# RWKV-7 recurrence in one core's trunk kernel: head pairs stacked on partitions, each product as two 64x64 matmuls in two quarters of the array

## The reference, cut to what matters

```python
def rwkv7_scan(r, w, k, v, a, b, s0):
    def step(s, xs):
        r_t, w_t, k_t, v_t, a_t, b_t = xs
        sa = jnp.einsum('bhvk,bhk->bhv', s, a_t)
        s = s * w_t[:, :, None, :] + sa[..., None] * b_t[:, :, None, :] + v_t[..., None] * k_t[:, :, None, :]
        return s, jnp.einsum('bhvk,bhk->bhv', s, r_t)
...
decay = jnp.exp(-jnp.exp(heads(w)))
o, s = rwkv7_scan(rh, decay, kh, vh, -kk, kk * ah, s0.astype(jnp.float32))
```

## Time and profile before

| what | value |
|---|---|
| median of 3 runs | 4238.09 us (4236.41 to 4239.77) |
| span of the profiled execution | 4230.9 us |
| TensorE busy in the span | 3786.5 us, 27818 matmul records |
| VectorE, ScalarE, GpSimd busy | 1979.8, 1070.2, 1270.0 us |
| RWKV stage: first scan to last state update | 2476.49 to 3037.74 us |

### The profile page before, as it was taken

How to read it: one execution, slowest core, us unless ns; L and a number is a source line. 1 busy time by engine, 2 the same in 40 slices (tenths; PEclk the granted TensorE clock), 3 DMA queues, 4 the chain that set the end, 5 groups by cost and what they waited for, 6 DMA issues and landing times. The chain is left out here.

```text
span 4230.9 us, 67031 instructions
## 1 busy us (share of the span) xinstructions
PE 3786.5 (89%) x27818; PEld 3609.9 (85%) x27818; DVE 1979.8 (47%) x2308; ACT 1070.2 (25%) x1429; POOL 1270.0 (30%) x685
## 2 busy tenths in 40 slices
PE   8997886989999998889978768888787999999988
PEld 7987876889999998889964458888786999999978
DVE  1653553455444456444122355555425445454573
ACT  2464332121111211310133432222303211111131
POOL 3334332433333333433320011111034333333342
PEclk9999998999999999999989889999998999999989
DMA  3110001111111111022210241111120111111111
GB/s 122 50 62 33 1 0 74 35 31 45 40 45 45 40 45 51 25 91 89 73 43 1 86 152 30 22 22 22 42 76 21 45 45 40 44 45 40 45 35 65
DMA packets 100906, 202.87 MB, mean 48 GB/s; under 512 B 59408, under 2 KB 60304, under 8 KB 99664
## 3 DMA queue, kind: packets, MB, share of 16 engines
q1 hardware_dynamic: 92928, 160.26, 12.2%
q10 hardware_dynamic: 7888, 41.33, 2.5%
HBM read 164.34 MB, written 37.23 MB: 48 GB/s over the span
## 5 line engine op out<-in xcount | busy, mean ns | idle before, releaser
L716 PE MATMUL PS<-XH,WHI 128*128 128x274 f32 x5248 | 1530.8, 292 | 93.6 <-DVE XL L2077 31.7
L716 PE MATMUL PS<-XL,WHI 128*128 128x274 f32 x5248 | 1528.5, 291 | 0.0
L716 PE MATMUL PS<-XH,WLO 128*128 128x274 f32 x5248 | 1525.9, 291 | 0.0
L716 PEld LDWEIGHTS PS<-XH,WHI 128*128 128x128 f32 x5248 | 998.8, 190 | 99.7 <-issue 45.8
L716 PEld LDWEIGHTS PS<-XL,WHI 128*128 128x128 f32 x5248 | 1000.6, 191 | 0.0
L716 PEld LDWEIGHTS PS<-XH,WLO 128*128 128x128 f32 x5248 | 999.5, 190 | 0.0
L810 POOL TENSOR_TENSOR WHI<-RAW,EPS 128x1024 fp32r<-128x1024 f32 x218 | 418.0, 1918 | 1871.0 <-PE PS L716 1829.2
L813 POOL TENSOR_TENSOR WLO<-RAW,WHI 128x1024 fp32r<-128x1024 f32 x218 | 571.1, 2620 | 17.1
L716 PE MATMUL PS<-HH,WHI 128*128 128x274 f32 x1408 | 411.4, 292 | 15.3 <-DVE HL L2102 13.1
L716 PE MATMUL PS<-HH,WLO 128*128 128x274 f32 x1408 | 409.0, 290 | 0.0
L716 PE MATMUL PS<-HL,WHI 128*128 128x274 f32 x1408 | 408.0, 290 | 0.0
(11 more groups left out here) (409 smaller groups left out, 5292.3 us busy)
## 6 DMA issues: line engine op xcount, KB each, us to landing
RAW<-in_units SPq DMA_DIRECT2D x218, 512.0 KB, 3.5
prepared_rows<-PREP SPq DMA_DIRECT2D x8, 1096.0 KB, 4.8
CIN<-prepared_rows SPq DMA_DIRECT2D x17, 512.0 KB, 4.5
c_rows<-DX ACTq DMA_DIRECT2D x14, 548.0 KB, 2.8
RKV<-c_rows SPq DMA_DIRECT2D x4, 1644.0 KB, 9.7
X<-in_x SPq DMA_DIRECT2D x8, 548.0 KB, 9.1
XR<-in_x ACTq DMA_DIRECT2D x1, 4384.0 KB, 18.3
x_rows<-Y ACTq DMA_DIRECT2D x1, 4384.0 KB, 12.9
```

The source lines that it names most:

```text
L716: last = nc.tensor.matmul(PS[:, 4 * slot + b, 0:width], wt[:, ring, w], r[:, k, b * width:(b + 1) * width], start=n == 0, stop=n == 3 * nk ...
```

## The change

Every `_B` tile becomes a stacked one, and the states too (`MB` has 4 x 64 columns instead of 4 x 128). A product of a pair is two matmuls of 64x64, one with the upper 64 partitions and one with the lower 64, each in its own quarter of the array, and the result is stacked in PSUM (128 x 256 for the four pairs, where it was 128 x 512). GpSimd has no part in the stage any more, and the zeros are gone. V is turned ahead of L instead of behind the level 0 block, into the PSUM bank that the b group takes later, so that the b group waits for ScalarE's copy of V. In front of each product stands a semaphore increment on TensorE's queue (`tiled`), which takes up the waits. The level masks are copied into a stacked tile, `PAIR_LEVEL`, once.

```diff
-        MB = [room("MB%d" % n, [128, 4, 128]) for n in range(2)]
+        MB = [room("MB%d" % n, [128, 4, 64]) for n in range(2)]
...
-            for h in range(2):
-                sp.dma_start(MB[1][half(h), :, half(h)], io["s_c"][half(h)]).then_inc(c_state_in, 16)
+            sp.dma_start(MB[1][:, :, :], io["s_c"]).then_inc(c_state_in, 16)
...
-                    sp.wait_ge(c_pool[p], C_POOL.at((i, 0), "v"))
+                    sp.wait_ge(c_pe[p], C_PE.at((i, 0), "vt"))
...
-            def c_blocks(out, lhs, rhs, more=()):
+            def c_heads(out, lhs, rhs, more=()):
                 terms = [(lhs, rhs)] + list(more)
                 for m in range(4):
                     for n, (l, r) in enumerate(terms):
-                        last = nc.tensor.matmul(out[:, m, :], l[:, m, :], r if len(r.shape) == 2 else r[:, m, :],
-                                                start=n == 0, stop=n == len(terms) - 1)
+                        for h in range(2):
+                            x = r[half(h), :] if len(r.shape) == 2 else r[half(h), m, :]
+                            last = nc.tensor.matmul(out[half(h), m, :], l[half(h), m, :], x,
+                                                    start=n == 0, stop=n == len(terms) - 1)
                 return last
+
+            def tiled():
+                pe.sem_inc(c_turn, 1)
...
                 if name == "prep2":
-                    pe.wait_ge(c_pool[p], C_POOL.at(j, "b"))
-                    c_blocks(per_head(b), A_B[p], B_B[p]).then_inc(s, 1)
+                    pe.wait_ge(c_dve[p], C_DVE.at(j, "scan"))
+                    tiled()
+                    c_heads(stacked(b + 3), CIN[p][:, 4:8, :], PAIR_ID).then_inc(s, 1)
+                    pe.wait_ge(c_dve[p], C_DVE.at(j, "bs"))
+                    tiled()
+                    c_heads(stacked(b), ARI[p][:, :, 0:64], B_S[p]).then_inc(s, 1)
                     pe.wait_ge(c_dve[p], C_DVE.at(j, "rs"))
+                    tiled()
                     for m in range(4):
-                        last = nc.tensor.matmul(k_group(p)[:, m // 2, 192 * (m % 2):192 * (m % 2) + 192], K_B[p][:, m, :],
-                                                ARI[p][:, m, :], start=True, stop=True)
+                        for h in range(2):
+                            last = nc.tensor.matmul(k_group(p)[half(h), m // 2, 192 * (m % 2):192 * (m % 2) + 192],
+                                                    K_S[p][half(h), m, :], ARI[p][half(h), m, :], start=True, stop=True)
                     last.then_inc(s, 1)
...
+                    pe.wait_ge(c_act[p], C_ACT.at(j, "vt"))
+                    tiled()
+                    c_heads(per_head(b + 3), B_S[p], ARI[p][:, :, 64:192]).then_inc(s, 1)
...
                 elif name[0] == "w":
                     pe.wait_ge(c_dve[p], C_DVE.at(j, "tt%d" % (level - 1) if level > 1 else "lm1"))
-                    c_blocks(per_head(b + 1), LM_B[p], TT_B[p]).then_inc(s, 1)
+                    tiled()
+                    c_heads(stacked(b + 1), LM_S[p], TT_S[p]).then_inc(s, 1)
...
                 elif name[0] == "w":
                     act.wait_ge(c_pe[p], C_PE.at(j, "lw%d" % level))
-                    nc.scalar.activation(W_B[p][:, :, :], per_head(4 * p + 1), ACT.Copy).then_inc(s, 1)
+                    nc.scalar.activation(W_S[p][:, :, :], stacked(4 * p + 1), ACT.Copy).then_inc(s, 1)
...
-                    for h in range(2):
-                        last = nc.vector.tensor_tensor(K_B[p][half(h), :, half(h)], k[half(h), :, :],
-                                                       PI_S[p][half(h), :, :], ALU.mult)
-                    last.then_inc(s, 1)
+                    nc.vector.tensor_tensor(K_S[p][:, :, :], k, PI_S[p][:, :, :], ALU.mult).then_inc(s, 1)
...
-            for x in ZEROED[9:]:
-                nc.vector.memset(x[:, :, :], 0.0)
+            nc.vector.memset(MB[0][:, :, :], 0.0)
+            for h in range(2):
+                nc.vector.tensor_copy(PAIR_LEVEL[half(h), :, :],
+                                      small("level", 6 * 128).rearrange("p (l c) -> p l c", l=6)[half(h), :, half(h)])
```

More of the change, by code:

```diff
@@ L378, in build @@
         RUN = room("RUN", [128, 256])
-        MB = [room("MB%d" % n, [128, 4, 128]) for n in range(2)]
+        MB = [room("MB%d" % n, [128, 4, 64]) for n in range(2)]
         behind_states = place[0]
         CIN = both("CIN", 24, 64)
-        A_B, B_B, K_B, V_B, LM_B, W_B, TA_B, TT_B, AK_B, BT_B, KT_B, VT_B = [both(x, 4, 128) for x in (
-            "A_B", "B_B", "K_B", "V_B", "LM_B", "W_B", "TA_B", "TT_B", "AK_B", "BT_B", "KT_B", "VT_B")]
         ARI = both("ARI", 4, 192)
-        B_S, PI_S, RB_S, RK_S = [both(x, 4, 64) for x in ("B_S", "PI_S", "RB_S", "RK_S")]
+        B_S, K_S, LM_S, W_S, TA_S, TT_S, AK_S, BT_S, KT_S, VT_S, PI_S, RB_S, RK_S, X_S, U_S = [both(x, 4, 64) for x in (
+            "B_S", "K_S", "LM_S", "W_S", "TA_S", "TT_S", "AK_S", "BT_S", "KT_S", "VT_S", "PI_S", "RB_S", "RK_S", "X_S", "U_S")]
         PX = both("PX", 4, 65)
-        U_B, X_B = K_B, W_B
-        ZEROED = [x[p] for x in (A_B, B_B, K_B, V_B, AK_B, BT_B, KT_B) for p in range(2)] + MB
+        PAIR_LEVEL = room("PAIR_LEVEL", [128, 6, 64])
         TAIL = SLAB // 32 * 32
@@ L1781, in c_step @@
                 elif name == "prep2":
+                    act.wait_ge(c_pe[p], C_PE.at(j, "vt"))
+                    nc.scalar.activation(VT_S[p][:, :, :], stacked(4 * p + 3), ACT.Copy).then_inc(s, 1)
                     act.wait_ge(c_pe[p], C_PE.at(j, "bg"))
                     act.wait_ge(c_dve[p], C_DVE.at(j, "rb"))
-                    for h in range(2):
-                        last = nc.scalar.activation(BT_B[p][half(h), :, half(h)], per_head(4 * p + 3)[half(h), :, 64:128],
-                                                    ACT.Copy, scale=-1.0)
@@ L1787, in c_step @@
-                    last.then_inc(s, 1)
+                    nc.scalar.activation(BT_S[p][:, :, :], per_head(4 * p + 3)[:, :, 64:128], ACT.Copy, scale=-1.0).then_inc(s, 1)
                     act.wait_ge(c_dve[p], C_DVE.at(j, "rk"))
-                    for h in range(2):
-                        last = nc.scalar.activation(
-                            KT_B[p][half(h), :, half(h)].rearrange("p (b m) n -> p b m n", b=2),
-                            k_group(p)[half(h), :, :].rearrange("p b (m n) -> p b m n", m=2)[:, :, :, 128:192], ACT.Copy)
@@ L1853, in _ @@
                 act.wait_ge(c_dve[p], C_DVE.at(j, "m"))
-                for h in range(2):
-                    act.dma_start(io[out][half(h)], MB[n][half(h), :, half(h)]).then_inc(c_state_out, 16)
-            act.wait_ge(c_state_out, 64)
+                act.dma_start(io[out], MB[n][:, :, :]).then_inc(c_state_out, 16)
+            act.wait_ge(c_state_out, 32)
             act.wait_ge(f_dve, F_DVE.at(3, "lo"))
@@ L2316, in c_step @@
                     nc.vector.scalar_tensor_tensor(RB_S[p][:, :, :], per_head(4 * p + 3)[:, :, 0:64], -1.0, pairs_of(upper),
                                                    ALU.mult, ALU.mult).then_inc(s, 1)
-                    for h in range(2):
-                        strict = small("pair_strict", 64)[half(h), :].unsqueeze(1).unsqueeze(1).to_broadcast([64, 2, 2, 64])
-                        last = nc.vector.tensor_tensor(
-                            AK_B[p][half(h), :, half(h)].rearrange("p (b m) n -> p b m n", b=2),
-                            k_group(p)[half(h), :, :].rearrange("p b (m n) -> p b m n", m=2)[:, :, :, 0:64], strict, ALU.mult)
@@ L2323, in c_step @@
[L2323 to L2327 removed]
+                    for out, first, mask in ((AK_S, 0, strict), (RK_S, 64, upper)):
+                        nc.vector.tensor_tensor(
+                            out[p][:, :, :].rearrange("p (b m) n -> p b m n", b=2),
+                            k_group(p).rearrange("p b (m n) -> p b m n", m=2)[:, :, :, first:first + 64],
+                            mask.unsqueeze(1).unsqueeze(1).to_broadcast([128, 2, 2, 64]), ALU.mult).then_inc(s, 1)
```

92 lines of the change are left out of this document (40 added, 52 removed).

## The result

The changed kernel takes 4039.2 us (median of 4 runs, 4035.1 to 4041.6) against 4238.5 for the kernel before on the same chip: a ratio of 0.9537, 95% interval 0.9524 to 0.9549. Forecast were 4002, with 3975 to 4185 as the range. The profiled execution took 4039.6 us, with a span of 4037.8. Of all executions behind this document one, of the later kernel `straight_mt`, took about twice the time of the others (7849.5 us); why isn't known, and its ratio is taken without it.

What follows compares the result with a forecast made beforehand. In the RWKV stage TensorE and the chain of waits were taken as near each other, TensorE ahead. 3669.6 us outside, a stage of 325 (sixteen pairs of 18.5 plus the ends) and 7.2 gave 4002 us; range 3975 to 4185.

Steps and rivals of the forecast that it cites:

- The quarters overlap: TensorE's products in the RWKV stage: both heads' quarters run at once, 0.467 us a group; chance 0.50.
- the quarters take turns: Rival for TensorE's products: 0.93 us a group, a pair 28.9 us, time 4180 us; chance 0.18, shared with the low clock.
- the LoRA products: Trace evidence: products on array rows 0 to 63 and 64 to 127 load and stream at the same time.
- The clock rival: TensorE falls to 1.2 GHz as each pass moves less through the array, about 4180 us; chance 0.18, shared with turns.
- The pair: Second half of one chunk beside the first half of the next: 18.5 us, sixteen times, 296 us in all.
- The walk: One pair in TensorE's order: 13.9 us of stream and 3.3 of eight gaps, none over 0.85, ending at 17.20.
- Markers: The 18 semaphore increments a pair on TensorE's queue: 0.07 us each, 1.3 us a pair.
- The last half: The lone last half of a chunk at the stage's end: 13 us.
- the lone first half: The first half of a chunk alone at the stage's start: 14 us, and 2 more for TensorE's cold start.
- the likeliest case's own range: With overlap as in the timed steps of a pair: 3975 (markers free) to 4050 us (0.2 us a marker, some low clock).
- a slow feed of the queue: Rival: TensorE's queue feeds the array too slowly, 0.8 us a group, time 4099 us; chance 0.20.

Runs made afterwards that it cites:

- straight_mt: The changed kernel with TensorE's loop written out and the transpose of LM_S put in the free half of the Gram product's bank: 3990.6 us, ratio 0.9421.
- same_rows: The changed kernel with TensorE's loop written out and both heads' matmuls on array rows 0 to 63, in different columns: 4147.9 us, ratio 0.9793.
- same_quarter: The changed kernel with TensorE's loop written out, all matmuls in one quarter of the array, head 0's first: 4570.0 us (one run).
- head_major: The changed kernel with TensorE's loop written out and, in every product, head 0's matmuls all ahead of head 1's: 4073.3 us, ratio 0.9619.
- act_blocks: The kernel before with the copies into A_B and B_B made by ScalarE in place of GpSimd: 4183.0 us against 4236.0, ratio 0.9875.

## Why the prediction was right, and where it was 37 us off

*The quarters overlap: right in size, half right in its reason.* Forecast were 0.467 us of stream for a product; measured are 0.47 to 0.48. kg (1.32) and bg (0.88) fit as well. The rival in which the quarters take turns fell, and with it the rule of the Trainium skill (TensorEngine Tiling (Array Packing), Restrictions and Gotchas) that different row tiles can't access one PSUM bank at once: here the two heads' tiles have different rows and write one bank, and they overlap at 0.029 us a record. They write different partitions of it; the same partitions weren't tried. My evidence, the LoRA products, made the rows the reason; `same_rows` shows that different columns serve as well. The clock rival (each pass moves less through the array) didn't happen in the changed kernel, which fills both row halves, but a clock of 0.50 did come in `same_rows` and `same_quarter`; the small passes alone weren't the reason, as `head_major` shows.

*The pair: right.* Forecast 18.5, measured 18.27 wherever no branch is in it. The walk's largest gap, at KT in front of the transpose, was 0.85 from stream to stream; the lines above give 2610.32 - 2608.81 - 0.47 = 1.04, with the marker in it (the profile's 0.85 counts from the last record's end). DVE at 0.41 to 0.43 and ACT at 0.38 are as read from the earlier trace rows. Markers were put at 0.07 for each product, 1.3 a pair. What one costs in this kernel wasn't measured; a second one costs nothing inside a stream, more than that behind a wait, and 0.04 to 0.057 on average. So the 18.5 is right as a sum, while its split into gaps and markers isn't shown.

*The ends: small errors.* The last half is 11.9 us and not 13. The first update comes 36.8 us after the first scan; less a pair of 18.3 this leaves 18.5 for the lone first half where I had 16. That part moves with the clock: the first update came after 36.8 us at a granted 0.82 here, and after 32.5 at 0.92 in `straight_mt`, which also has one wait less.

*GpSimd: right that it goes.* The prediction put no price on it alone; the 25 to 45 us of the later forecast were too low, for its replacement gains 53 us by itself. It was paid twice, by the wait and by the clock behind it.

*A reading that was off.* The 128x274 projections were said to hold nearly all of TensorE's busy time. The profile has 2661 of the 3786.5 us on their line (L716), which is 70%; the stage has 473. Nothing in the sum rests on it.

*The step that failed: "A pair: 18.5 us" times sixteen.* The sum held one length for all pairs and no term for the code. I doubled the count of matmuls and priced only the array's time for them, not the instructions as something that has to be fetched. In six pairs the branch waits, the queue runs dry a second time and the clock falls: 153.1 - 6 x 18.27 = 43.5 us. Without them the stage would be 322.8 and not 325. The rest of the account: outside the stage 3671.5 for 3669.6, and 1.4 us between span and median where I had added 7.2. So 4002 + 41.3 + 1.9 - 5.8 = 4039.4, the measured time within its spread. That it still falls into the likeliest case's own range (to 4050) is luck in part: the upper end stood for dearer markers and some low clock, not for the code.

That it is the code's length is shown from both sides: written out, 36.3 of the 43.5 us go; a long loop of old products has the same branch of 3.6 us and the same repeated fetches. That the branch waits for the fetch itself, and not for something that goes with it, is inferred from the packets. What stays open: how much code is kept (two old pairs are, four aren't), and whether the 1.8 to 3.3 us that the written-out kernel still loses in each of four pairs are the fetch alone.

The forecast named a slow feed of the queue as a rival, at 4099 us. It was near in kind, but wrong in place: in a stream the queue feeds the array at 0.029 us a record without loss; it starves behind the branch back.

## What to carry to other kernels

When a change multiplies the instructions of an engine's loop, price the code too: look at the branch's own duration and at the packets of the instruction queue, before and after, turn by turn. If they recur, write the loop out or make it shorter; how much is lost depends on how far the queue runs ahead of its engine. Split products into quarters so that neighbours in the queue lie in different ones. And a wait on the path is worth more than its length when the clock falls behind it: price both, and look whether a shared buffer, and not data, is what is waited for.

## What the runs showed of the hardware that I had not expected

- TensorE's branch back took 0.21 us with 432 matmul records in the loop, and 3.3 to 3.8 with 864; the array was idle for 1.7 us of it with full-array products, and for 3.0 to 3.3 and then 1.7 to 2.4 with quarters.
- Two 64x64 matmuls that share their rows and not their columns overlap as fully as diagonal ones: 0.053 us a record at half the clock, against 0.107 in one quarter (0.029 for diagonal ones at the full clock).
- With operands in the upper 64 rows alone, the granted clock stayed at 0.50 (1.2 GHz) for the whole stage at 98% busy; with both halves in use it was 1.00 (2.4 GHz) at 84%.
- Waits of 1.80 us in each pair left the clock at 1.00 in `act_blocks`; waits of 3.14 in the same place had the product behind them at half speed.
